# First layer of a two-block network: projections as seven half-size products, head loads issued two a step

## The reference, cut to what matters

```python
proj = jnp.einsum('bsd,df->bsf', h, w_in).astype(jnp.float32)
qa, ka, va, qb, kb, vb, lr_f, lr_b, gate = _split(
    proj, (512, 512, 512, 512, 512, 1024, 16, 16, 1536))
oa = dilated_attention(heads(qa, 8), heads(ka, 8), heads(va, 8), rel_bias)   # three dilations, band of 64
ob = bidirectional_gated_scan(qh, kh, g_f, kh, g_b, heads(vb, 4))            # gates from lr_f, lr_b
y = jnp.concatenate([oa, ob], axis=-1) * jax.nn.silu(gate)
```

## Time and profile before

| | us |
|---|---|
| median of three runs | 4033.66 |
| the profiled execution | 4034.02 |
| its span | 4032.3 |
| TensorE busy in it | 3549.7 (88%) |
| VectorE, ScalarE, GpSimd busy | 1846.1, 1082.7, 1183.1 |
| mean granted TensorE clock | 0.931 of 2.4 GHz |

### The profile page before, as it was taken

The page is one execution under the profiler, slowest core; times in us unless marked ns, Lnnn a source line. Parts: engine busy times, 40 slices in busy tenths (PEclk is TensorE's granted clock), DMA queues, the critical chain, the costliest instruction groups (busy, mean ns, idle before and its releaser), DMA issues. The chain is left out here.

```text
span 4032.3 us, 47003 instructions
## 1 busy us (share of the span) xinstructions
PE 3549.7 (88%) x16369; PEld 2313.2 (57%) x16369; DVE 1846.1 (46%) x4038; ACT 1082.7 (27%) x2206; POOL 1183.1 (29%) x948
## 2 busy tenths in 40 slices
PE   8989998999798999999996798998867776949996
PEld 4635676778344677577556347574457775524442
DVE  1025552444573376676774450324479476240011
ACT  1023343432341232333432450221114112111111
POOL 0000000243343455555664452002212544211110
PEclk9999999999898999999998896998988887969998
DMA  3264542231532111211212533123324713347996
GB/s 117 64 183 144 143 148 71 82 116 56 220 147 63 58 57 42 69 57 41 74 39 102 214 118 78 41 74 96 123 72 149 253 66 115 120 178 245 322 315 232
DMA packets 409824, 494.01 MB, mean 123 GB/s; under 512 B 70514, under 2 KB 314506, under 8 KB 409603
## 3 DMA queue, kind: packets, MB, share of 16 engines
q1 hardware_dynamic: 380983, 457.42, 34.2%
q0 software_dynamic: 4608, 16.78, 1.6%
q10 hardware_dynamic: 24012, 16.97, 1.3%
HBM read 362.32 MB, written 128.77 MB: 122 GB/s over the span
## 5 line engine op out<-in xcount | busy, mean ns | idle before, releaser
L821 POOL TENSOR_TENSOR hgrn_queries<-hgrn_qd,hgrn_pair_decay 128x640 f32<-128x640 f32 x192 | 263.8, 1394 | 291.5 <-PE hgrn_ps_a L936 251.6
L871 PE MATMUL hgrn_ps_w<-xT,hgrn_ring 128*128 128x512 f32 x432 | 196.8, 602 | 1.8 <-PEq L34 1.8
L395 PE MATMUL gla_bg_ps<-gla_bg_w,xT 128*128 128x256 f32 x768 | 186.5, 387 | 4.7 <-DMA gla_bg_w<-in_w_in_ab_dram 4.7
L1475 PE MATMUL end_ps_z<-end_w,end_yT 128*128 128x512 f32 x384 | 166.9, 594 | 1.9 <-DMA end_w<-in_w_out_ab_dram 1.2
L2579 PE MATMUL end_ps_z<-end_w,end_yT 128*128 128x512 f32 x384 | 167.2, 595 | 0.8 <-ACT end_yT L2507 0.8
L395 PEld LDWEIGHTS gla_bg_ps<-gla_bg_w,xT 128*128 128x128 f32 x768 | 144.8, 193 | 35.6 <-issue 10.6
L391 PE MATMUL att_bg_ps<-xT,att_bg_w 128*128 128x512 f32 (+1 forms) x288 | 136.4, 613 | 13.3 <-POOL att_ident L1782 13.3
L45 POOL MEMSET gla_ident<- 128x128 f32 x1 | 0.2, 204 | 484.1 <-POOLq L34 484.1
L1041 DVE TENSOR_TENSOR hgrn_k_end<-hgrn_kd,hgrn_end_decay 128x128 f32<-128x128 f32 x168 | 136.0, 848 | 9.2 <-issue 2.6
L871 PEld LDWEIGHTS hgrn_ps_w<-xT,hgrn_ring 128*128 128x128 f32 x432 | 81.8, 194 | 94.7 <-issue 94.5
L871 PE MATMUL hgrn_ps_w<-hgrn_xs,hgrn_wsum 128*128 128x512 f32 x288 | 130.6, 601 | 4.5 <-ACT hgrn_sig L1155 4.5
(11 more groups left out here) (644 smaller groups left out, 7721.3 us busy)
## 6 DMA issues: line engine op xcount, KB each, us to landing
expw_wg<-in_exp_w_gate_dram SPq DMA_DIRECT2D x16, 2048.0 KB, 9.9
expw_wu<-in_exp_w_up_dram SPq DMA_DIRECT2D x16, 2048.0 KB, 16.3
expw_wd<-in_exp_w_down_dram SPq DMA_DIRECT2D x16, 2048.0 KB, 21.8
att_w_ada<-in_ada_w_dram SPq DMA_DIRECT2D x24, 1024.0 KB, 6.2
hgrn_ring<-in_w_in_c_dram SPq DMA_DIRECT2D x18, 1024.0 KB, 5.4
end_gt<-gate_l SPq DMA_DIRECT2D x16, 768.0 KB, 8.5
hgrn_ring<-in_w_in_c_dram SPq DMA_DIRECT2D x24, 512.0 KB, 5.5
hgrn_o<-hgrn_o_stage SPq DMA_DIRECT2D x192, 64.0 KB, 1.6
```

Source lines behind the costliest of these rows:

```text
L395: last = pe.matmul(bank[0:job.rows, q * job.width:(q + 1) * job.width], job.acts[:, k, t * P:t * P + job.rows], w[:, k, 0:job.width], star ...
L821: pool.tensor_tensor(queries[:, d, s, :].rearrange("p (b a c) -> p b a c", b=POINTS, a=PC), q, f, ALU.mult).then_inc(queries_done, 1)
L871: last = pe.matmul(bank[:, :], a[:, k, :], x(k), start=(fresh and k == 0), stop=(k == HK - 1), skip_group_check=True)
L1475: made = pe.matmul(ps_z[h][:, :], yT[:, k, :], w[:, k, h * BANK:(h + 1) * BANK], start=(k == 0), stop=(k == NB - 1))
```

## The change

Every unit of 256 weight columns is split in halves along input channels, weight columns and tokens, and computed with seven products of halves in place of eight (Strassen's scheme in Winograd's form). A fill is now one such half product: four products of 512 columns (CHANNEL) or sixteen of 128 columns (TOKEN, where it was 256). GpSimd makes four sums of weights a unit (`sums`), one over half of the weights in the ring itself; VectorE makes four sums of the activations once, one of them in `xT` itself, which `low_rank_scan` undoes. Of the seven results four are moved by ScalarE and three are joined on VectorE by an addition. A store is now 128x512 elements.

In `project_halves`, which takes the place of `project`, stores are issued by SP, `low` is computed first, and the first two units of the attention's background are loaded ahead. In the attention LEAD is twelve (smaller) fills and comes ahead of the wait for `consts`; `bg.sums(pool, 0)` comes ahead of the constants; the head loads are issued two a step, first between the fills of the lead, then in the steps of the pair before; `w_ada` has two buffers for three, `row` one for two, and the exps are written over `s_sb`, so that `p_sb` goes.

```diff
         sb = lambda n, s, d=F32: ctx.enter_context(nc.sbuf_tensor(f"{tag}_{n}", s, d))
         sem = own_semaphores(nc, ctx, tag)
@@ -75,15 +74,17 @@
         def _(sp):
             for t in range(T):
                 sp.dma_start(raw[:, t, :], src[t * P:(t + 1) * P, :]).then_inc(raw_loaded[t], 16)
+            rows = weights.rearrange("(k p) n -> p k n", p=P)
+            sp.dma_start(low_w[:, :, :], rows[:, :, low_at:low_at + 2 * RANK]).then_inc(w_loaded, 16)
             for b in range(2):
-                sp.dma_start(wbuf[b][:, :, :], weights.rearrange("(k p) n -> p k n", p=P)[:, :, b * W:(b + 1) * W]).then_inc(w_loaded, 16)
+                sp.dma_start(ring[:, b, :, :], rows[:, :, b * UNIT_W:(b + 1) * UNIT_W]).then_inc(w_loaded, 16)
             with nc.allow_non_contiguous_dma(reason="a vector goes down the partitions"):
                 sp.dma_start(cond[:, 0, :], c[0].rearrange("(k p) -> p k", p=P)).then_inc(cond_loaded, 16)
                 sp.dma_start(cond[:, 1, :], c_ctx.rearrange("(k p) -> p k", p=P)).then_inc(cond_loaded, 16)
...
+class Halves:
+
+
+
+    HK = KB // 2
+    ROLE = {SNAP1: 0, PLAIN: 1, SNAP21: 0, SNAP22: 2, JOIN22: 0, JOIN21: 2, LAST: 0}
+    PLACE = {SNAP1: 0, PLAIN: 0, LAST: 2, SNAP21: 1, JOIN21: 1, SNAP22: 2, JOIN22: 2}
+    ROW_COL = {PLAIN: (0, 0), LAST: (0, 1), JOIN21: (1, 0), JOIN22: (1, 1)}
+    BY_DVE = (PLAIN, JOIN22, JOIN21)
+    FRESH = (SNAP1, PLAIN, SNAP22)
+    DONE = (PLAIN, JOIN22, JOIN21, LAST)
...
+    def load(self, sp, u):
+        unit = self.units[u]
+        if u >= self.RING:
+            sp.wait_ge(self.filled, 7 * (u - self.RING) + 7)
+        src = unit.weights.rearrange("(k p) n -> p k n", p=P)[:, :, unit.col:unit.col + UNIT_W]
+        sp.dma_start(self.ring[:, u % self.RING, :, :], src).then_inc(self.w_loaded[u % self.RING], 16)
...
+    def transfer(self, sp, g):
+        self.put(sp, g)
+        self.fetch(sp, g)
...
+    def sums(self, pool, u):
+
+        a, s = self.weights_of, self.wsum
+        wait(pool, self.w_loaded[u % self.RING], self.loads_by[u])
+        wait(pool, self.filled, 7 * u)
+        pool.tensor_tensor(s[:, 0, :, :], a(u, 0, 0), a(u, 1, 0), ALU.subtract).then_inc(self.s_made, 1)
+        pool.drain()
+        pool.tensor_tensor(a(u, 1, 0), a(u, 1, 0), a(u, 1, 1), ALU.add).then_inc(self.s_made, 1)
+        pool.drain()
+        pool.tensor_tensor(s[:, 1, :, :], a(u, 1, 0), a(u, 0, 0), ALU.subtract).then_inc(self.s_made, 1)
+        pool.drain()
+        pool.tensor_tensor(s[:, 2, :, :], a(u, 0, 1), s[:, 1, :, :], ALU.subtract).then_inc(self.s_made, 1)
...
+    def multiply(self, pe, g, x_made=None):
+        for f, lo, hi in self.work[g]:
+            u, i = self.fills[f]
+            bank, w, x = self.ps[self.bank_of[f]], self.stationary(u, i), self.x[i]
+            if lo == 0:
+                if i == SNAP1:
+                    wait(pe, self.w_loaded[u % self.RING], self.loads_by[u])
+                e = self.before_on[f]
+                if e is not None:
+                    pe.wait_ge(self.added if self.fills[e][1] in self.BY_DVE else self.moved, self.nth[e])
+                if x_made is not None and u == 0 and i in (SNAP21, JOIN22, JOIN21):
+                    pe.wait_ge(x_made, {SNAP21: 2, JOIN22: 3, JOIN21: 4}[i])
+                if i in (SNAP21, LAST):
+                    pe.wait_ge(self.s_made, 4 * u + (3 if i == SNAP21 else 4))
+            for n in range(lo, hi):
+                q, k = n // self.HK, n % self.HK
+                if self.units[u].kind == CHANNEL:
+                    last = pe.matmul(bank[:, :], w[:, k, :], x(k), start=(i in self.FRESH and n == 0), stop=(k == self.HK - 1), skip_group_check=True)
+                else:
+                    last = pe.matmul(bank[:, q * P:(q + 1) * P], x(k)[:, q * P:(q + 1) * P], w[:, k, :],
+                                     start=(i in self.FRESH and n == 0), stop=(k == self.HK - 1), skip_group_check=True)
+            if hi == self.count(f):
+                last.then_inc(self.filled, 1)
+
+    def move(self, act, g):
+
+        for f, end in enumerate(self.ended_in):
+            u, i = self.fills[f]
+            if end != g - 1 or i in self.BY_DVE:
+                continue
+            place = self.PLACE[i]
+            act.wait_ge(self.filled, f + 1)
+            wait(act, self.stored[place], 16 * {SNAP22: 2 * u, LAST: 2 * u + 1}.get(i, u))
+            act.activation(self.stage[:, place, :], self.ps[self.bank_of[f]][:, :], ACT.Copy).then_inc(self.moved, 1)
+
+    def join(self, dve, g):
+
+        for f, end in enumerate(self.ended_in):
+            u, i = self.fills[f]
+            if end != g - 1 or i not in self.BY_DVE:
+                continue
+            into = self.stage[:, self.PLACE[i], :]
+            snap = f + {PLAIN: SNAP1, JOIN22: SNAP22, JOIN21: SNAP21}[i] - i
+            dve.wait_ge(self.filled, f + 1)
+            dve.wait_ge(self.moved, self.nth[snap])
+            dve.tensor_tensor(into, self.ps[self.bank_of[f]][:, :], into, ALU.add).then_inc(self.added, 1)
...
+        @block.sync
+        def _(sp):
+            seven.load(sp, 2)
+            sp.wait_ge(low_moved, 2)
+            sp.dma_start(low_out, low[:, :, :].rearrange("p s t -> p (s t)")).then_inc(low_stored, 16)
+            for g in range(seven.slots):
+                seven.transfer(sp, g)
+                for n, unit in enumerate(ahead):
+                    if g == 7 * (len(units) - 3 + n) + 7:
+                        sp.wait_ge(seven.filled, g)
+                        src = unit.weights.rearrange("(k p) n -> p k n", p=P)[:, :, unit.col:unit.col + UNIT_W]
+                        sp.dma_start(ring[:, n, :, :], src).then_inc(ahead_loaded, 16)
+            seven.end(sp)
+            sp.wait_ge(low_stored, 16)
+            sp.wait_ge(ahead_loaded, 16 * len(ahead))
+
+        @block.gpsimd
+        def _(pool):
+            for u in range(len(units)):
+                seven.sums(pool, u)
+
+        @block.tensor
+        def _(pe):
+            for s in range(2):
+                for k in range(KB):
+                    last = pe.matmul(ps_l[s][0:2 * RANK, :], low_w[:, k, :], xT[:, k, s * BANK:(s + 1) * BANK], start=(k == 0), stop=(k == KB - 1))
+                last.then_inc(low_made, 1)
+            for g in range(seven.slots):
+                seven.multiply(pe, g, x_made)
+
+        @block.vector
+        def _(dve):
+            x = lambda k, s: xT[:, k * HK:(k + 1) * HK, s * BANK:(s + 1) * BANK]
+            dve.tensor_tensor(xs[:, 0, :, :], x(1, 1), x(0, 1), ALU.subtract).then_inc(x_made, 1)
+            dve.drain()
+            dve.tensor_tensor(xs[:, 1, :, :], xs[:, 0, :, :], x(0, 0), ALU.add).then_inc(x_made, 1)
+            dve.wait_ge(low_made, 2)
+            dve.tensor_tensor(x(0, 1), x(0, 1), x(0, 0), ALU.subtract).then_inc(x_made, 1)
+            dve.drain()
+            dve.tensor_tensor(xs[:, 2, :, :], x(1, 0), xs[:, 1, :, :], ALU.subtract).then_inc(x_made, 1)
+            for g in range(seven.slots + 1):
+                seven.join(dve, g)
+
+        @block.scalar
+        def _(act):
+            for s in range(2):
+                act.wait_ge(low_made, s + 1)
+                act.activation(low[:, s, :], ps_l[s][0:2 * RANK, :], ACT.Copy).then_inc(low_moved, 1)
+            for g in range(seven.slots + 1):
+                seven.move(act, g)
 ...
-    LEAD = 6
+    LEAD = 12
...
+            def load_some(j, turn):
+
+                for n in range(2 * turn, min(2 * turn + 2, LOADS)):
+                    load(j, n)
...
             def load_ada(u):
-                wait(sp, weighted, u - 2)
+                wait(sp, weighted, u - 1)
...
-                if s == ST - 1 and j + 2 < HEADS:
-                    sp.wait_ge(o_made, ST * (j + 1))
-                    load(j + 2)
-
-            bg.begin(sp)
+                if s == 0 and 0 < j and j + 1 < HEADS:
+                    sp.wait_ge(o_made, ST * j)
+                if j + 1 < HEADS and s < LOADS // 2:
+                    load_some(j + 1, s)
+
+            bg.load(sp, 2)
+            load_ada(0)
             sp.wait_ge(consts, 1)
...
         def _(pool):
+            bg.sums(pool, 0)
             make_identity(pool, ident)
...
-            pe.wait_ge(consts, 1)
             for g in range(LEAD):
                 bg.multiply(pe, g)
+            pe.wait_ge(consts, 1)
             score(0)
...
-                wait(dve, p_done, g - 1)
+                wait(dve, p_turned, g - 1)
...
             dve.wait_ge(consts, 1)
+            for g in range(LEAD):
+                bg.join(dve, g)
             for g in range(HEADS * ST):
...
                 if g > 1:
                     move_out(g - 2)
+                bg.join(dve, LEAD + g)
...
+            low_rows = slice(0, KB // 2)
+            dve.tensor_tensor(xT[:, low_rows, BANK:SEQ], xT[:, low_rows, BANK:SEQ], xT[:, low_rows, 0:BANK], ALU.add).then_inc(restored, 1)
             dve.wait_ge(consts, 1)
```

(35 more changed lines are left out.)

181 lines of the change are left out of this document (132 added, 49 removed).

## The result

The changed kernel takes 4005.5 us (median of five runs, 4003.5 to 4014.2), the kernel before 4033.7: a ratio of 0.9934 (95% interval 0.9923 to 0.9945), so 28 us less. A later series of runs of the same two kernels gave 0.9919 (0.9903 to 0.9936). The forecast was 3997, its range 3972 to 4020: the side and the range hold, and the gain is 8 to 9 us smaller than the forecast's.

What follows compares the result with a forecast made beforehand. TensorE was taken as the bound inside the attention, with pauses at its entry. The terms +1.5 - 5.6 - 8.7 - 7.4 - 38.7 + 22 = -36.9, from 4034.0, gave 3997 us, range 3972 to 4020.

Steps and rivals of the forecast that it cites:

- Prologue, +1.5: Before the first projection: one more 128 KB load is waited for, costing 1.5 us, bounds 0.4 to 3.
- Price of a product: TensorE's products: 0.86 us for 512 columns, 0.433 for 256, 0.2225 for 128, taken from the earlier trace.
- first projection, -5.6: The projection ahead of the attention: 167.9 us falls to 162.3, with the new sums on VectorE and GpSimd covered.
- rival D: Token fills: weight loads stop hiding in sixteen 128-column products in a row, so the kernel is slower, up to 4103; chance 0.08.
- Hand-over, -8.7: Between projection and attention: TensorE's pause falls to 4.6 us, with smaller stores, weights ready and no wait for the constants.
- End of the lead, -7.4: First score to first transpose: 11.7 us falls to 4.3, as no store holds ScalarE; bounds 0 and 9.
- Rival C: Attention entry: the pauses stay, from late head loads or a store holding ScalarE; 16 us lost, 4013; chance 0.08.
- Inside the attention, TensorE, -38.7: Background products in the attention: TensorE's time falls from 193.4 to 154.7 us through fewer and cheaper fills.
- What that meets, +22: Attention: new TensorE waits on VectorE, 16 us from joins, 3 from steps with a total, 3 from sums and late loads.
- rival A: Attention: the joins cost nothing that counts, as VectorE's delays do not reach TensorE; -59, 3975; chance 0.13.
- B: Attention: the loop through VectorE becomes the bound, costing 61 us at worst; about 4016 at half the excess; chance 0.13.
- Scan, 0: Scan entry: VectorE's 3.4 us undoing of the sum lies beside TensorE's wait for small loads, so nothing changes.

Runs made afterwards that it cites:

- The experiment on the kernel before: Kernel before with only the attention's entry reordered: TensorE's lead ahead of its wait for constants, second pair's loads and two ada loads after the lead's stores; 4018.6 us.

## Why the prediction was right, and where it was off

**Prologue, +1.5: was +0.4.** The share of the stretch's bandwidth (0.4) was nearer the price, and the landing alone (2.4) was the wrong neighbour. The load landed after 10.0 us and the stretch grew by 0.4, and by 0.3 to 1.0 in the other kernels that have it (26.1 to 26.8 us): here the load's latency lies beside the others' and only a small part of it is paid.

**Price of a product and first projection, -5.6: was -5.0.** TensorE's timeline in a token unit answers to the earlier trace rows and to rival D:

```profile
181.62 3.74 PE L562 MATMUL in_ps<-l_ring,l_xs 128*128 128x128 f32 x32
185.20 3.74 PE L562 MATMUL in_ps<-l_wsum,xT 128*128 128x128 f32 x32
...
192.93 7.26 PE L560 MATMUL att_bg_ps<-xT,l_ring 128*128 128x512 f32 x10 [4.00 <-PEq L34]
```

Sixteen products in 3.58 us, 0.224 each, where the step of four gave 0.2225; the loads of 0.19 stay hidden in a whole fill. The stage lasts 162.7 us against the forecast's 162.3, with GpSimd's 24 sums and VectorE's joins all covered. D is refuted. The rule of the Trainium skill's page "TensorE: Matmul & The Clock Gate" that was weighed there stands in its section "The mechanism", which also lets a load into the background weight buffer be pulled ahead. Taken as the prediction took it, it would have made these stretches 9.6 us each, an estimate from the 0.6 us a product; they are 3.6, and the measurement decides.

**Hand-over, -8.7: was -9.3.** The last row above has a pause of 4.0 us; 4.6 were forecast. The prediction's own terms (0.6, 2.7 and 0.9) add up to 4.2, so most of the difference is a slip in its sum. The experiment on the kernel before parts the 9.3: 4.6 from going ahead of the constants, 2.5 from weights that lie ready, and 2.2 from the shorter way to the barrier.

**End of the lead, -7.4: was -8.6.** The chain from score to transpose takes 3.1 us and not 4.3. ScalarE's timeline shows the step that failed:

```profile
224.72 1.09 ACT L576 ACTIVATE l_stage<-att_bg_ps 128x512 f32<-128x512 f32 x2 [14.45 <-DMA qb<-l_stage]
...
234.32 1.28 ACT L2162 ACT_TABLE_LOAD   x1
238.97 0.51 ACT L2162 ACTIVATE att_s_sb<-att_s_sb,att_shift 128x256 f32<-128x256 f32 x1 [3.37 <-DVE att_shift L2119]
```

The table load, 1.28 us, which the forecast had in the chain, is done 3.4 us ahead of the first exp, since ScalarE was free to run on to it. A store still holds ScalarE, for 14.5 us, but early in the lead, and it has caught up more than ten us before the exps. Rival C is out: no load was late, and the store's wait reached nobody.

**Inside the attention, TensorE, -38.7: was -34.4.** Summed from the distances of starts, the background's pieces take 200.2 us before and 165.8 after, 34.4 less; 4.3 are missing. The three pieces at the lower clock lost 4.4, and the one before some 0.9, so the clock explains about 3.5 of them. In the kernel with join and sums moved, where no piece is slow, the pieces take 161.4, which is 38.8 less than before. The prices of the fills were right; that pauses of 1 to 2 us could bring the clock down was not in the sum, though the prediction had named a slow clock after each pause for the entry.

**What that meets, +22: was +25.8** (44.8 to 70.6 us from transposes to score). Joins: 16 forecast in 19 steps, 17.1 in 18. This is the step on which the forecast rested, and it held to 1 us; rival A (nothing reaches TensorE) falls with it, and so does B (every join in full, late loads). Sums and late loads: 3 forecast, 7.2 measured, all of it sums, since no `ada` load was waited for. The reason given for the low end was the failing step: "the bias reads only one SBUF operand" held for the bias (a mean of 0.37 us in both kernels), but not for the shift behind it, which waited out a whole sum, and the bias stands behind the weighings of the step before, which were blocked too. The 7.2 lie inside the bounds of 0 to 12. The Trainium skill's page "SBUF — State Buffer", section "SBUF: two separate sides", has the two engines lock each other out for a whole instruction, and names two cases on VectorE's side: two SBUF inputs, and a mode that uses both ports. The trace agrees for the first (2.85 us added to three weighings beside three sums). The prediction reasoned from the first alone; the shift, with one input, was held as well, and no row shows in which mode it ran. The rest, a `total` in the step, 3 forecast: 2.7 with all other causes, 1.3 of that being there before.

So the attention was to gain 16.7 and gained 9.1. Of the 7.6 missing, 4.3 are TensorE's own time (mostly the clock), 4.2 the sums and 1.1 the joins, and the others gave back about 2.

**Scan, 0: was +1.1** up to the gate. Not explained (above).

Put together: entry 2.0 better than the forecast, attention 7.6 worse, scan and behind 2.9 worse, 8.5 in all, which is the difference of 3997 and 4005.5. The forecast's mechanism was right, two costs were too small (the clock and the sums), and three of the entry's were too large (the first load, the way to the barrier, the table load). And most of the waits that it counted as the price of the form were the price of one line's place: of the 25.8 us measured, 16 went when the join stood behind the bias, and 17.5 us of the attention with them.

## What to carry to other kernels

When work is added to an engine that has time left, ask in which place of its order it stands: 20 joins of 0.69 us each ahead of the one result that the bound engine waits for cost it 17 us, and behind that result almost nothing. GpSimd work on SBUF is not free beside VectorE's; put it where VectorE's delayed work has no reader, and count that even a two-element instruction beside it can last as long as GpSimd's own (1.15 us here for 0.17). Before crediting a new form of the arithmetic with a gain, make the reordering that comes with it on the old kernel: here it was about half.

## What the runs showed of the hardware

Not expected by the prediction was how far the blocking between GpSimd and VectorE goes. A shift of two elements on each partition, with SBUF operands only, took 1.15 us beside a sum, against 0.17. It goes the other way as well, at the entry of the scan in after:

```profile
659.82 2.29 DVE L2531 TENSOR_TENSOR xT<-xT 128x2048 f32<-128x2048 f32 x1 [5.89 <-PEq L34]
...
660.18 2.08 POOL L47 TENSOR_SCALAR_AFFINE_SELECT gla_ident<-gla_ident 128x128 f32<-128x128 f32 x1 [0.19 <-issue]
```

GpSimd's select takes 2.08 us and ends with VectorE's sum; with that sum on 8 elements it took 0.29:

```profile
663.87 0.29 POOL L47 TENSOR_SCALAR_AFFINE_SELECT gla_ident<-gla_ident 128x128 f32<-128x128 f32 x1 [0.19 <-issue]
```

The second surprise is the clock inside a stretch that is 94% busy: pauses of 1 to 2 us on TensorE were followed, three times, by some 3 us at a granted clock of 0.51 to 0.56, which adds about 1.4 us each, nearly as much as the pause itself. Two executions of the same attention had three and five such pieces, so one profile doesn't give their number.
